# Second mixer: the forget row is added to the scores by one float32r pass over its upper and lower parts

## What is computed

```python
def _fox(q, k, v, log_f):
    F = jnp.cumsum(log_f, axis=1).transpose(0, 2, 1)
    def block(i):                       # 128 queries
        ...
        logits = (jnp.einsum('bqhd,bkhd->bhqk', qb, k).astype(jnp.float32) * dh ** -0.5
                  + Fq[..., None] - F[:, :, None, :])
        logits = jnp.where(causal[None, None], logits, -jnp.inf)
        p = jax.nn.softmax(logits, axis=-1)
        return jnp.einsum('bhqk,bkhd->bqhd', p.astype(v.dtype), v)
```

## Time and profile before

| | |
|---|---|
| median of 3 runs | 1849.62 us (1846.66 to 1850.04) |
| the profiled execution's own time | 1848.67 us |
| its span, first to last instruction | 1846.8 us |
| PE busy | 1811.4 us, 98% |
| DVE, ACT, POOL busy | 1367.5, 1145.3, 108.2 us |
| mean granted TensorE clock | 0.991 of 2.4 GHz |

### The profile page before, as it was taken

The page is one execution under the profiler, slowest core; times in us unless marked ns, Lnnn a source line. Parts: engine busy times, 40 slices in busy tenths (PEclk is TensorE's granted clock), DMA queues, the critical chain, the costliest instruction groups (busy, mean ns, idle before and its releaser), DMA issues.

```text
span 1846.8 us, 25078 instructions
## 1 busy us (share of the span) xinstructions
PE 1811.4 (98%) x9475; PEld 1514.4 (82%) x9475; DVE 1367.5 (74%) x1283; ACT 1145.3 (62%) x1169; POOL 108.2 (6%) x78
## 2 busy tenths in 40 slices
PE   9999999999999999999999999999999999889998
PEld 7897888888878888888888888888888878778887
DVE  3755555543568888888888888888888888966555
ACT  4544554544547777777777777777777773445444
POOL 0002000100030000000000000000000002110000
PEclk9999999999999999999999999999999999999999
DMA  9834556542379999999999999999999993335551
GB/s 283 290 108 140 184 190 194 174 145 73 134 231 378 374 359 371 375 374 373 352 381 380 360 372 375 373 374 351 381 378 360 372 376 118 115 118 189 183 183 45
DMA packets 255492, 502.53 MB, mean 272 GB/s; under 512 B 14572, under 2 KB 97045, under 8 KB 255054
## 3 DMA queue, kind: packets, MB, share of 16 engines
q1 hardware_dynamic: 248000, 474.67, 72.7%
q0 software_dynamic: 6528, 26.35, 4.6%
q10 hardware_dynamic: 910, 0.76, 0.1%
HBM read 493.86 MB, written 12.62 MB: 274 GB/s over the span
## 4 chain that ended last, share of the span: by engine, by line
PE 89%; DVE 5%; ACT 2%; POOL 2%; issue 1%; DMA 1%; DVEq 0%; POOLq 0%; SPq 0%; ACTq 0%
PE psum L581 23%; PE psum L583 23%; PE psum L584 23%; PE psum L790 9%; PE psum L792 5%; DVE psum L2169 2%; PE psum L1088 1%; PE psum L671 1%; POOL wl L2263 1%; PE psum L702 1%; ACT wh L1231 1%; DVE x L1719 1%; DVE ta L2169 1%; DVE wl L1655 0%; POOL rstd L2254 0%
## 5 line engine op out<-in xcount | busy, mean ns | idle before, releaser
L1655 DVE TENSOR_TENSOR wl<-ring,wh 128x2048 fp32r<-128x2048 f32 x443 | 1014.3, 2291 | 265.9 <-ACT wh L1231 264.6
L1231 ACT ACTIVATE wh<-ring 128x2048 fp32r<-128x2048 f32 x450 | 862.1, 1916 | 283.3 <-PE psum L581 181.6
L581 PE MATMUL psum<-wh,xT 128*128 128x512 f32 (+1 forms) x1136 | 434.5, 382 | 2.5 <-DVE wl L1655 1.1
L584 PE MATMUL psum<-wh,xT 128*128 128x512 f32 (+1 forms) x1136 | 425.5, 375 | 0.0
L583 PE MATMUL psum<-wl,xT 128*128 128x512 f32 (+1 forms) x1136 | 425.4, 375 | 0.0
L581 PE MATMUL psum<-wh,wnh 128*128 128x512 f32 x672 | 266.7, 397 | 1.5 <-DVE wnl L1811 1.5
L583 PE MATMUL psum<-wl,wnh 128*128 128x512 f32 x672 | 264.0, 393 | 0.0
L584 PE MATMUL psum<-wh,wnl 128*128 128x512 f32 x672 | 263.9, 393 | 0.0
L581 PEld LDWEIGHTS psum<-wh,xT 128*128 128x128 f32 x1136 | 215.5, 190 | 46.5 <-issue 6.2
L790 PE MATMUL psum<-xT,wh 128*128 128x512 f32 x704 | 249.1, 398 | 0.4 <-DVE xT L1665 0.4
L584 PEld LDWEIGHTS psum<-wh,xT 128*128 128x128 f32 x1136 | 215.1, 189 | 39.8
(11 more groups left out here) (298 smaller groups left out, 1452.0 us busy)
## 6 DMA issues: line engine op xcount, KB each, us to landing
ring<-in_w_moe SPq DMA_DIRECT2D x336, 1024.0 KB, 6.6
ring<-in_w_dense SPq DMA_DIRECT2D x33, 1024.0 KB, 5.3
ring<-in_w_in_ab SPq DMA_DIRECT2D x14, 1024.0 KB, 11.2
ring<-in_w_in_cd SPq DMA_DIRECT2D x12, 1024.0 KB, 5.2
ring<-in_w_gate SPq DMA_DIRECT2D x11, 1024.0 KB, 5.3
ring<-in_w_up SPq DMA_DIRECT2D x11, 1024.0 KB, 5.3
ring<-in_w_down SPq DMA_DIRECT2D x11, 1024.0 KB, 4.9
ring<-in_w_in SPq DMA_DIRECT2D x10, 1024.0 KB, 7.9
```

Source lines behind the costliest of these rows:

```text
L581: last = pe.matmul(o, a[0], b_[0], start=first, stop=False)
L584: return pe.matmul(o, a[1], b_[0], start=False, stop=final)
L1231: act.activation(upper_half[i], ring[:, u_, :], ACT.Copy).then_inc(hi_ready[s_], 1)
L1655: dve.tensor_tensor(lower_half[i], ring[:, u_, :], upper_half[i].bitcast(F32), ALU.subtract)\
```

## The change

The forget row is split as the weights are: a float32r upper part and the rest. Both go, with the selector of ones, into a new float32r tensor `forget_r` that lies over `gA`, where `rowsel` was. For the first head of a pair the upper parts of the eight rows stand on partitions 0 to 7 and the lower ones on 32 to 39, for the second head on 64 to 71 and 96 to 103. One float32r matmul on 40 partitions adds both parts; its tile is 64 partitions, like that of the score matmul ahead of it. ScalarE writes the upper parts (two copies of 8 x 256) ahead of the old copy `nfT`; VectorE subtracts to get the lower parts (two of 8 x 256), behind its `lower` for unit w = 4. The constant that POOL loads grows from 8 x 1024 to 104 x 768 elements. The fillers and the two waits ahead of unit w = 3 are gone; PE now waits for the constant and for VectorE's subtractions (`forget_low`) ahead of the first scores, in the middle of that unit.

```diff
-        rowsel = gaf[0:8, 0:8 * P].rearrange("p (h t) -> p h t", h=8)
+        rowsel = forget_r[0:104, 0:4 * P].rearrange("p (h t) -> p h t", h=4)
+        forgets = forget_r[0:104, 4 * P:4 * P + T]
...
                     if forget:
-                        last = pe.matmul(o, rowsel[:, 2 * hp + hh, :], nfT[:, 0:n], start=False, stop=True)
+                        last = pe.matmul(o, rowsel[HD * hh:HD * hh + 40, hp, :], forgets[HD * hh:HD * hh + 40, 0:n],
+                                         start=False, stop=True)
...
+                    if s == 0:
+                        pe.wait_ge(late_in, 16)
+                        pe.wait_ge(forget_low, 2)
                     if s < 8:
                         group_scores(CD_FIRST + s, tq, tk, forget=True)
...
                     last.then_inc(step_done, 1)
-                    keep_busy(8, 0)
-                    pe.wait_ge(step_evac, steps[0])
-                    pe.wait_ge(late_in, 16)
...
                 if w == 2:
-                    act.activation(nfT, step_out()[0:8, 0:T], ACT.Copy, scale=-1.0).then_inc(step_evac, 1)
+                    ps = step_out()
+                    act.wait_ge(late_in, 16)
+                    for r in (0, HD):
+                        act.activation(forgets[r:r + 8, :], ps[0:8, 0:T], ACT.Copy, scale=-1.0)
+                    act.activation(nfT, ps[0:8, 0:T], ACT.Copy, scale=-1.0).then_inc(step_evac, 1)
+                    assert steps[0] == STEPS_FORGET
...
             lower()
+            dve.wait_ge(step_evac, STEPS_FORGET)
+            for r in (32, HD + 32):
+                dve.tensor_tensor(forgets[r:r + 8, :], nfT, forgets[0:8, :].bitcast(F32), ALU.subtract).then_inc(forget_low, 1)
             for w in range(3, 12):
...
-            pool.dma_start(rowsel[:, :, :], c_rowsel).then_inc(late_in, 16)
+            pool.dma_start(forget_r[0:104, :], c_rowsel.bitcast(F32R)).then_inc(late_in, 16)
...
-    rowsel = np.zeros((8, 8, P), np.float32)
+    rowsel = np.zeros((104, 4 * P + T), np.float32)
     for h in range(8):
-        rowsel[h, h] = 1
+        for row in (HD * (h % 2) + h, HD * (h % 2) + 32 + h):
+            rowsel[row, h // 2 * P:(h // 2 + 1) * P] = 1
```

More of the change, by code:

```diff
@@ L49 @@
 STEPS_ROUTER = 39
+STEPS_FORGET = 28
 CONSTS = 16 * 7
@@ L193, in build @@
         ngc = sb("ngc", [P, 2, 8])
+        ga_at = nc.sbuf_base
         gA = sb("gA", [P, 4, 384])
+        forget_r = nc.alloc_sbuf_tensor_at("forget_r", [P, 4 * P + T], F32R, offset=ga_at)
         small = sb("small", [P, 256])
@@ L313, in build @@
         ls_b = sem("log_sigmoid_ready")
+        forget_low = sem("forget_lower")
         gla_neg = sem("gla_negated")
```

## The result

The changed kernel takes 1835.51 us (median of six runs) against 1848.44 us for the kernel before beside it: ratio 0.9923, 95% interval 0.9907 to 0.9939. Two later measurements of the same pair give 0.9935 [0.9918, 0.9952] and 0.9944 [0.9928, 0.9961]. One of the first six runs (2279.53 us) was slow and is left out of the ratios and of what follows; without it the median is 1835.00. Over all series of runs the median is 1848.37 us for 44 runs of before (1844.13 to 1852.96) and 1835.35 us for 15 of after (1833.35 to 1839.23), a gain of 13.0 us; the forecast was 1833.0.

The account below looks back on a forecast made before the run. PE (TensorE), busy 98% of the span, was taken as the bound. Start of the mixer -0.3, passes -11.7 and clock -4.6 sum to -16.6 us, from 1849.62 to 1833.0; range 1830 to 1841.5.

Parts of the forecast that it names:

- The passes: Second mixer's eight forget groups: half-tile float32r passes cut them from 16.6 to 4.9 us, -11.7 (bounds -4.4 to -11.7).
- rival A: The forecast itself: both heads of a forget group run side by side, clock up, 1833.0 us; chance 0.45.
- B: Forget groups: second head's scores begin only once first head's forget pass is issued; 7.0 us in all, 1835.1; chance 0.25.
- C: Forget groups: no overlap of heads, groups as costly as the first mixer's masked ones, 1840.3 us; chance 0.17.
- The start of the mixer: Before the first scores: fillers and a wait go, a 1.70 us wait for VectorE comes; -0.3 us.
- The clock: Second mixer: three stretches at granted clock 0.50 expected to go, -4.6 us (bounds 0 and -4.6).
- Nothing given back: Behind the shorter groups: PE waits for nothing new, and everything after the mixer shifts as a whole.
- The constant: POOL's selector transfer in the first layer grows from 32 to 312 KB but stays hidden: 0 us.
- D: Passes shrink as in rival A, but low-clock stretches remain or move to the pause: 1837.6 us; chance 0.08.
- E: Forget passes: 40-partition float32r takes as long as fp32, nothing but 0.3 us saved: 1849.3; chance 0.03.
- F: Slower: narrow groups plus the pause pull the clock down at the pause and all eight groups, 1854.1 us; chance 0.02.

Follow-up runs that it names:

- full-tile form: Changed kernel with the float32r forget pass on the full array (all 104 partitions) instead of half of it: 1842.52 us, 6.9 above the changed kernel.

## Why the prediction was right where it was, and wrong where it was

**The passes: right, by rival A's mechanism.** Forecast 16.6 to 4.9, measured 16.64 to 5.00, a term of -11.64 for -11.7. The two heads' scores start together, and a head's forget pass does not hold up the other head. B, strict order, gave groups of 0.69 and 1.06, measured are 0.49 and 0.76, and the row of three L676 records ahead of the first L681 refutes it: the second head's first record starts ahead of a matmul that stands before it in the list. By the Trainium skill's page that I weighed ("TensorE: Matmul & The Clock Gate", Part 3), it would not. C is what the full-tile form shows, 12.14 us, and is the price of the wrong tile, not of the added pass. What I took from the earlier trace rows (the shape decides, not the presence of a second matmul) was the step that carried the number.

**The start of the mixer: right in kind, 0.2 too large.** Forecast a pause of 1.70 and the first score 0.26 us earlier; measured 1.84 and 0.06 (5.93 us after the sum, 5.99 before). VectorE's pair took 0.86, not the 0.75 of the earlier trace rows. The single subtraction is not the longer: in nanoseconds, least, median and most (lines of the queries by source, the first of after, the second of before from 337 to 338),

```profile
L2020 DVE TENSOR_TENSOR forget_r<-gnat,forget_r x2: 415/416/418, 398.9 to 399.3; 8x256 fp32r<-8x256 f32 x2
L1832 DVE TENSOR_TENSOR tk<-tk x2: 418/418/419, 337.2 to 337.5; 128x256 f32<-128x256 f32 x2
```

So 8 partitions cost as much as 128, and float32r as much as float32. What differs is when the second one starts: 0.45 us after the first here, 0.34 in the earlier trace rows, where it overlaps the first. Why was not tried. The release took 0.10 instead of 0.05. Not seen was that the wait could be dodged altogether: VectorE had been idle for 3.48 us ahead of its pass.

**The clock: the step that was mis-sized.** I took three low stretches in one trace for a property of the groups and put -4.6 on their going. Nothing at 0.50 was found in the mixer of any changed form, but in three of four executions of before there was nothing either, so it is not shown that the change takes them away. The mean of the four is 0.75 of a stretch, 1.1 us, and -11.7 - 1.1 = -12.8 against 13.0 of the pooled medians. That these lie so near is no proof: four traces are few, and the first and last parts differ by up to 4.3 and 2.7 us from one execution to the next. Shown are the 11.7 us in the mixer; where the other 1.3 come from stays open. That the forecast lay 2.5 us too low is mostly this term, 3.5 too large, less the 1.2 us by which the median of the first three runs lay above that of 44; that the two errors had opposite signs was luck. What stands ahead of a stretch in one trace is no proof of a cause: the same eight groups at the same lengths ran at 1.00 three times. Even in that one trace the link was loose: the third stretch, from 439.8, began 1.2 us behind the end of a group of 256 keys (436.11 + 2.50), and the fourth such group, at 444.24, had none behind it. I had seen that low stretches elsewhere "may fall otherwise" and granted them 2 us; the same doubt belonged to the three that I counted.

**Nothing given back: right in the mixer, with a loss elsewhere in the profiled pair.** PE waits for nothing from 400 to 442 and through the expert loop. In the first pair 1.7 of the 16.5 us went again in the last block. Before, its last low stretch there lies partly on a wait (2.79 us busy of 3.30), after, a low stretch lies on dense work (3.40 of 3.40):

```profile
1624.40:1627.70 3.30, 2.79 (x12) 2.42 (x12) 2.73 (x7) 0.07 (x1) 0.52 (x1) 0.50 0.00 0
```
```profile
1613.90:1617.30 3.40, 3.40 (x10) 2.63 (x9) 3.37 (x4) 1.26 (x2) 0.00 (x0) 0.50 0.02 5
```

The second trace of after has its stretches elsewhere (1564.6, 1591.9 and 1609.0) and a rest that is 2.0 us shorter, so this too differs from execution to execution, and no effect of the change shows in it (1388.0 to 1390.0 in the four traces of before, 1387.7 to 1390.3 in the three of after).

**The constant, D, E and F.** The constant costs nothing that shows: the first part takes 393.9 to 395.8 us in after and 394.2 to 398.2 in before. No low stretch lay at the pause (D). E's 1849.3 and F's 1854.1 lie 10 us and more above 1839.23, the highest of the 15 times of after.

**Open.** Why the clock falls in the mixer in one execution of before and not in three. It was not tried whether it can do so in the changed kernel; nine traces of it and its forms have none there, nor has the one of before with its scores adjacent. With one in four for before, none in ten is too little to tell a difference.

## What to carry to other kernels

When matmuls of 64 partitions pair up on the two halves of the array, give whatever stands between them the same tile shape, or put it behind both: each change of shape cost 0.2 us here, and a longer contraction padded with zeros on the right tile (40 partitions) was far cheaper than a short one on another (8): 0.65 us against 1.66 for a float32 group of 128 keys. Before you count a low stretch of the clock as a saving, profile the same kernel a few times and count only what is in each trace. Where a small result is wanted soon, put its copies ahead of the large work on each engine that makes it; here that was worth 1.9 us in the mixer part, and moving PE's wait past half a unit 0.8.

## What the runs showed of the hardware that I had not expected

- A matmul on one half of the array starts ahead of one that is earlier in PE's list and belongs to the other half (three score records of two heads start between 399.84 and 400.03, the first head's forget pass at 400.06).
- The same program shows none or three stretches at a granted clock of 0.50 in one 60 us part, 1.5 us of loss each, and the execution with three had fewer elsewhere, so its total was in the middle of the others (spans of 1845.6 to 1847.6 us in the four traces).
- A float32 pass of 40 partitions behind scores of the same tile shape costs 0.23 us for two heads at 128 keys and 0.44 at 256, the float32r pass 0.07 and 0.13; behind a change of shape the float32 pass cost 0.41 and 0.63 for one head.
- A subtraction of 8 x 256 on VectorE takes as long as one of 128 x 256, 0.42 us.
